# Sink as a score column, queries split at the projection, and one fp32r mask matmul in windowed attention

## The reference

```
s_loc = jnp.einsum("bnqkgd,bnjkd->bnkgqj", qb, kb) * scale
s_loc = jnp.where(valid[None, :, None, None], s_loc, NEG_INF)
s_ctx = jnp.einsum("bnqkgd,bjkd->bnkgqj", qb, kc) * scale
p = jax.nn.softmax(jnp.concatenate([s_loc, s_ctx, sink_l], axis=-1), axis=-1)
o = p[..., :nloc] @ vb + p[..., nloc:nloc + nctx] @ vc
```

## Time and profile before

| | |
|---|---|
| median of 3 runs | 2837.03 us |
| profiled execution | 2846.73 us, span 2844.8 us |
| TensorE busy | 2609.6 us (92%), 13096 matmuls |
| VectorE busy | 1161.8 us (41%) |
| ScalarE busy | 1112.5 us (39%) |
| GpSimd busy | 1289.8 us (45%) |
| mean granted TensorE clock | 0.965 |

### The profile page before, as it was taken

How to read it: one execution, slowest core, us unless ns; L and a number is a source line. 1 busy time by engine, 2 the same in 40 slices (tenths; PEclk the granted TensorE clock), 3 DMA queues, 4 the chain that set the end, 5 groups by cost and what they waited for, 6 DMA issues and landing times.

```text
span 2844.8 us, 40046 instructions
## 1 busy us (share of the span) xinstructions
PE 2609.6 (92%) x13096; PEld 2133.8 (75%) x13096; DVE 1161.8 (41%) x2014; ACT 1112.5 (39%) x2334; POOL 1289.8 (45%) x1012
## 2 busy tenths in 40 slices
PE   7788969888999999999999869888999899999998
PEld 2787957766887778888887368767888778888886
DVE  2443344399153323324332355496244233323332
ACT  2634552377221443334332342576212433333332
POOL 1557962255222255556554132354222455556553
PEclk9889989999999999999999979999998999999999
DMA  6335651100121043344335431000120233344333
GB/s 228 87 113 175 190 175 56 34 1 1 46 63 39 23 124 112 108 124 154 111 111 215 157 125 45 23 1 13 51 60 25 65 116 108 111 132 144 111 109 120
DMA packets 387923, 270.53 MB, mean 95 GB/s; under 512 B 15452, under 2 KB 360668, under 8 KB 385252
## 3 DMA queue, kind: packets, MB, share of 16 engines
q1 hardware_dynamic: 373792, 231.26, 27.0%
q10 hardware_dynamic: 14024, 37.88, 3.8%
HBM read 259.63 MB, written 9.45 MB: 95 GB/s over the span
## 4 chain that ended last, share of the span: by engine, by line
PE 55%; issue 19%; POOL 13%; DVE 9%; ACT 3%; DMA 1%; POOLq 0%; DVEq 0%; SPq 0%; ACTq 0%
PE ps L576 54%; POOL w_lo L490 13%; DVE a_probT_lo L1317 2%; DVE a_q_split L1317 1%; DVE softmax_stats L1496 1%; DVE a_out_sum L1317 1%; PE ps L721 1%; ACT a_probT_hi L1097 1%; DVE norm_tmp L1397 1%; DVE hT_lo L1317 0%; DVE softmax_stats L1317 0%; ACT a_prob L1087 0%; DVE softmax_stats L1503 0%; DMA w_ada<-in_w_ada 0%; DVE r_prev L1608 0%
## 5 line engine op out<-in xcount | busy, mean ns | idle before, releaser
L490 POOL TENSOR_TENSOR w_lo<-w_raw,w_hi 128x512 fp32r<-128x512 f32 x786 | 1051.9, 1346 | 1130.9 <-ACT w_hi L953 1121.2
L576 PE MATMUL ps<-hT_hi,w_hi 128*128 128x512 f32 (+1 forms) x2528 | 950.1, 376 | 49.5 <-POOL w_lo L490 26.1
L576 PE MATMUL ps<-hT_lo,w_hi 128*128 128x512 f32 (+1 forms) x2528 | 939.0, 371 | 0.0
L576 PE MATMUL ps<-hT_hi,w_lo 128*128 128x512 f32 (+1 forms) x2528 | 938.5, 371 | 0.0
L953 ACT ACTIVATE w_hi<-w_raw 128x512 fp32r<-128x512 f32 x786 | 492.2, 630 | 1071.7 <-PE ps L576 896.5
L576 PEld LDWEIGHTS ps<-hT_hi,w_hi 128*128 128x128 f32 x2528 | 487.0, 193 | 141.5 <-POOL w_lo L490 21.6
L576 PEld LDWEIGHTS ps<-hT_hi,w_lo 128*128 128x128 f32 x2528 | 487.3, 193 | 79.7
L576 PEld LDWEIGHTS ps<-hT_lo,w_hi 128*128 128x128 f32 x2528 | 487.6, 193 | 76.5
L1317 DVE TENSOR_TENSOR merge_tmp<-merge_tmp,ps 128x512 f32<-128x512 f32 (+1 forms) x160 | 101.5, 634 | 684.9 <-PE ps L576 608.7
L527 POOL TENSOR_TENSOR a_prob<-a_prob,softmax_stats 128x640 f32<-128x640 f32 (+2 forms) x144 | 163.4, 1135 | 177.6 <-DVE softmax_stats L1516 177.6
L1317 DVE TENSOR_TENSOR merge_tmp<-merge_tmp 128x512 f32<-128x512 f32 (+1 forms) x120 | 182.5, 1521 | 4.1
(11 more groups left out here) (187 smaller groups left out, 2919.3 us busy)
## 6 DMA issues: line engine op xcount, KB each, us to landing
w_raw<-in_w_in SPq DMA_DIRECT2D x512, 256.0 KB, 2.9
w_raw<-in_w_o_rest SPq DMA_DIRECT2D x120, 256.0 KB, 2.7
w_ada<-in_w_ada SPq DMA_DIRECT2D x16, 1536.0 KB, 9.5
w_raw<-in_w_out SPq DMA_DIRECT2D x80, 256.0 KB, 3.0
w_raw<-in_w_o_attn SPq DMA_DIRECT2D x40, 256.0 KB, 2.8
w_raw<-in_dft_x SPq DMA_DIRECT2D x32, 256.0 KB, 2.8
rope<-in_rope ACTq DMA_DIRECT2D x4, 1024.0 KB, 5.0
gate_row<-gate_rows ACTq DMA_DIRECT2D x5, 512.0 KB, 3.5
```

Source lines behind the costliest of these rows:

```text
L490: eng.tensor_tensor(w_lo[:, r, :], raw[:, r, :], w_hi[:, r, :].bitcast(F32), ALU.subtract).then_inc(sem["w_split"], tally.up("w_split"))
L576: return eng.matmul(dst, lhsT, rhs, start=start, stop=stop)
```

## The change

Three things are changed together.

1. The sink becomes a column of the scores. ScalarE copies the sink of the head into PSUM beside the scores of step `n + 2`, right after the exponential of step `n`, to the right of the scores or, in every second pair of steps (`left`), to the left; there the probabilities start at element 1 of their tile. The maximum (written negated by the reduction) and the exponential with its sum then cover the sink too. The small VectorE operations `total` and `bias`, the exponential of the sink and the negated copy of the sink go. The scale is applied when the query tiles are evacuated, not in the exponential. TensorE's scores wait for `sink_col` instead of `prob`.
2. Queries are split into halves as each query tile is projected: VectorE writes the rotary sum in place, ScalarE copies the high halves ahead of its next evacuation, VectorE subtracts. All heads' halves stay in SBUF (`q_first`, `q_next`, `q_last`), so attention has no split of queries.
3. Both mask triangles are added by one fp32r matmul of 256 columns with a strided output; at the first and last block it is one of 128 columns.

More of the change, by code:

```diff
@@ L720, in turn @@
                             eng.wait_ge(sem["probT_saved"], tally.now("probT_saved", 1))
-                        last = eng.transpose(ps[:, bank, col:col + P], prob[:, n % 4, j * P:(j + 1) * P], ident[:, :])
+                        last = eng.transpose(ps[:, bank, col:col + P], prob[:, n % 4, left(n) + j * P:left(n) + (j + 1) * P], ident[:, :])
                     last.then_inc(sem["probT"], tally.up("probT"))
@@ L910, in _ @@
                 pe_goes_on(eng, tally)
[L911 removed]
+                eng.wait_ge(sem["prob"], tally.take("prob", p.NT * HEADS))
                 project(p, 8)
@@ L1112, in attention @@
                                ACT.Copy).then_inc(sem["a_split_high"], tally.up("a_split_high"))
-                queries(0)
-                queries(1)
-                groups = len(steps) // 4
+                sink_column(0)
+                sink_column(1)
                 exps(0)
```

84 lines of the change are left out of this document (28 added, 56 removed).

## The result

The changed kernel takes 2799.28 us (median of 4 runs, 2795.84 to 2799.94) where the kernel before took 2837.82 in the same comparison: ratio 0.9864, 95% interval 0.9846 to 0.9882. A second comparison gave 2797.91 us and 0.9847 (0.9834 to 0.9860). So it is 38 to 42 us faster; 2806 was predicted, in a range of 2783 to 2827.

What follows compares the result with a forecast made beforehand. Bound: TensorE over most of the span; in attention a chain alternating between engines, VectorE holding some gaps. Inner groups 19, end groups 4, starts 3.4, context about 5: 31 us in all, from median 2837.0 to 2806, range 2783 to 2827.

Steps and rivals of the forecast that it cites:

- Gap B: Gap between steps' last transposes, with values and query split: 3.15 falls to TensorE's own 2.6 us, 0.55 per group.
- Gap A: Gap between steps' last transposes, with the half addition: 2.5 falls to 2.2 us as VectorE loses bias and sum.
- Mask: Mask matmul in the attention steps: taken at +0.0, far bound +0.13 us a step, twice per group on the chain.
- Odd starts: GpSimd's scaling where probabilities begin one element later, two of four steps: factor 1 taken, bounds 1 and 2.2.
- rival D: GpSimd's scaling of odd-start steps becomes the bound: at 5 us a group takes 12.5, total 2884 us; chance 0.05.
- Projection: Behind each query tile: sum, two ScalarE copies, two VectorE subtractions, done 1.0 us before the next tile; costed at nothing.
- rival C: Query projection: ScalarE copies push weight splits late, each of eight tiles costs 2 to 2.5 us; 2830 to 2837; chance 0.09.
- Context pass: Attention pass of 16 steps, one head on 128 queries each: about 5 us off, bounds 2 and 8.
- Start: Start of each of three attentions, where TensorE began after four query splits: 1.1 us off each, 3.4 in all.
- rival A: Attention: the 2.2 gap becomes the loop's 1.98 and attention starts at full clock; 54 us off, 2783; chance 0.13.
- Rival B: Gap with the query split: next reduction lands before the low half, 3.15 falls only to about 2.9; 2822; chance 0.15.
- D: Gap between steps' last transposes, with values only: TensorE's own work, 2.6 us in the forecast group.

Runs made afterwards that it cites:

- the values moved: Changed kernel with the value products put ahead of the last transpose, and low half, half addition and gate one step later: 2790.18 us, ratio 0.9821.

## Why the prediction was right

*The mechanism and its place.* The gain came from the attentions, from VectorE's low half coming sooner, as predicted. Predicted 31 us, found 35.5 to 37.4 there. By steps:

- *Gap B, queries:* predicted 0.55 us off. With the sink part in place it was 0.47, alone 0.60. Right, and the new floor was TensorE's own work.
- *Gap A, sink:* predicted 2.5 - 0.28 = 2.2; found 2.36. The step that failed is the price. The 0.16 and 0.12 of the chain end at 1911.03, where the low half starts, so these 0.28 us hold the reciprocal too, which stays and takes 0.08 of them; what goes is the distance of the other two in the queue, 0.07 + 0.13 = 0.20. "More important, the exponential no longer queues" was wrong: with the queue's 0.20 accounted for, the 32 us of waiting that came back without the sink part cost no gap of an inner group anything.
- *Only one of the four steps has them on the chain:* true beside the query part, not by itself. In the kernel before, gap B had them too (0.19).
- *Mask:* predicted 0, found 0.07 us off in each of two steps, outside my bounds: I had allowed for a loss only. The nearest row priced the mask product rightly (0.12), though its sixteen matmuls include the two bf16 mask products themselves; what shrank were the products behind it. The rule of fast loading from the Trainium skill's page "TensorE: Matmul & The Clock Gate" (section on Fast Weight Load), by which the time would rise, did not come to bear: the trace agrees that the fp32r identity loads slower (0.19 us against 0.10 for the bf16 one), but the load lies under the product before it, as the row had said.
- *Sink copy:* taken at 0.28, bounds 0 and 0.28. It takes 0.171 us on average (24.4 us for 144), near the 0.19 estimated from the Trainium skill's page "ScalarE: Activation LUTs", and doubling it costs nothing.
- *Odd starts:* factor 1, right; rival D never came up. GpSimd's scaling in the second x pass:

```profile
L547 POOL TENSOR_TENSOR a_prob<-a_prob,softmax_stats x58: 1037/1252/1263, 1799.4 to 1928.6; 128x640 f32<-128x640 f32 x48, 128x512 f32<-128x512 f32 x10
```

  Half of the 48 full ones start at element 1, and the slowest took 1263 ns, the median 1252. The bound of 2.2 was read too freely: the two rows differ in their operation too (multiply and add against multiply alone), and in the same convolution the scalar_tensor_tensor that reads the same tile from element 3 takes 1284 ns, as the one that reads it from element 2. That the odd start made the 2.2 is not shown.
- *Projection:* cost nothing, right, and rival C is out. VectorE's last subtraction of a tile starts at 460.9 and ends near 462.1, the next tile is evacuated from 461.8 to 462.8 (so VectorE is done 0.7 us before the next tile is there; 1.0 was forecast), and four evacuations lie 10.9 us apart:

```profile
L970 ACT ACTIVATE proj_raw<-ps x4: 1023/1027/1028, 461.8 to 494.5; 128x1024 f32<-128x1024 f32 x4
...
L1343 DVE TENSOR_TENSOR a_q_split<-proj_raw,a_q_split x2: 1218/1220/1221, 459.7 to 460.9; 64x1024 fp32r<-64x1024 f32 x2
```

  For the context pass, where I had 0.5 us per tile as a bound (and 1.5 us in an expectation above), the attention starts at 95.0 to 97.0 us in the kernels with the split in the projection and at 95.7 to 96.8 in those without: nothing that shows.
- *Context pass:* predicted about 5 us and 1.1 for its start, found 4.4 to 4.5 with its start.
- *Start:* predicted 1.1 us each. From the copy of the context keys to the first scores it was 549.0 to 552.24 = 3.2 us and is 541.44 to 543.78 = 2.3, so 0.9. Not in the forecast, but half met by rival A: the stretch at the granted clock of 0.50 (1.2 GHz) that follows was not avoided, yet it became shorter. Windows of the changed kernel (granted clock last but two; the earlier trace rows is before):

```profile
542.00:547.00 5.00, 2.62 (x11) 2.36 (x11) 2.43 (x5) 2.65 (x8) 0.00 (x0) 0.66 0.01 3
547.00:552.00 5.00, 4.83 (x26) 4.46 (x27) 2.71 (x7) 3.45 (x11) 3.12 (x3) 0.65 0.00 0
552.00:557.00 5.00, 4.61 (x39) 4.17 (x38) 4.16 (x11) 4.04 (x13) 3.12 (x3) 1.00 0.00 0
```

  (1 - 0.66) and (1 - 0.65), times two, times 5 us make 6.9 us at half clock; windows of 1 us give 6.8, and before 10.2. What these 3.4 us are worth can be read inside one kernel, where one x pass had the short stretch and the other the long one. That is so without the sink part, without the query part, with the values moved and with the mask twice: with the long stretch the first half addition comes 0.8, 0.9, 0.6 and 0.9 us later; where both passes have the short one it is 0.0 to 0.2 us apart. So the shorter stretch gives 0.6 to 0.9 us in each of the two passes.

The sum was 31 us; the attentions gave 35.5 to 37.4 and the totals 38 to 42. By its terms, from the distances between half additions: the 24 inner groups gave 22.9 us (19 forecast), of which the mask is 3. The starts and outer groups of the two x passes gave 10.1 (6.2 forecast); 1.3 of it is chance, the last group at half clock in the profile of before, and 1.2 to 1.8 the shorter stretches at half clock. The context pass gave 4.4 (6.1 forecast). That the forecast group of 9.43 us so nearly meets the 9.39 of the kernel without the mask part is in part luck: A was forecast 0.16 too short, while B and D, the latter read as 2.6 where the rows give 2.54, were forecast 0.04 and 0.08 too long, and 0.05 was added for slack.

Rival B, that the low half still stands behind a reduction, is out: B is 2.48. The statement that TensorE is next in line held, but only in half of the gaps, where the doubled mask shows it.

## What to carry to other kernels

Follow one repeated marker of the bounding engine through one period, write down its gaps, and ask for each gap who ends it; a part of a change is worth what it takes off a gap it ends, and two parts that shorten the same gap are not worth their sum. Price small operations by the distance between starts in their queue, not by their duration, and do not price a wait on an engine that has time. Where the bounding engine waits at one point and has independent work just behind it, move that work ahead of the wait and spread it over the steps: here that took off another 24 us where the whole change had taken 38 to 42.

## What the runs showed of the hardware

- One-element operations on VectorE last 0.14 to 0.21 us in the trace, but the next one starts 0.07 us later (0.13 behind the bias, a tensor_scalar) in the runs without the sink part and with two reciprocals. The Trainium skill's page "Vector Engine (DVE) Microarchitecture Reference", section "Measured stream behaviour on trn2", gives about 75 ns per instruction after queue overlap for longer streams. The trace agrees for the sum and the reciprocal and not for the bias; by that figure the two operations of the sink part would have been priced at 0.15 us as an estimate, where 0.20 was measured. Two one-element copies from SBUF into PSUM on ScalarE last 0.27 us together.
- Two fp32r products of 256 columns take 0.31 us behind a pair of bf16 products and 0.24 behind an fp32r one. Whether the type or the weight load with less time under the products before it is the cause is not shown.
- fp32r weight loads of 128x128 last 0.19 us while products of 256 columns follow one another at 0.12: the loads run under the products. In the changed kernel the mask's load starts with the product of 384 columns before it.
- The stretch at half clock at the start of an x attention added up to 6.8 us in 17 of the 20 x passes of kernels with the queries split in the projection (10.2 in the other three), and to 10.2 us in seven of the eight passes of kernels without. What decides between the two is not shown.
- The last group of an x pass took 7.0 to 7.2 us at full clock and 8.3 to 8.9 in the six passes where the granted clock fell to 0.50 in it. What decides that is not shown either.
